# A decoder block on one core: the MLP split into an up phase and a down phase, the down projection by Strassen's seven block products

## What is computed

```python
x = x + rms_norm(mixed, norm_mix_post[l])
h2 = rms_norm(x, norm_mlp_pre[l])
a = jax.nn.relu(h2 @ w_up[l])                              # (512, 2048) @ (2048, 8192)
x = x + rms_norm((a * a) @ w_down[l], norm_mlp_post[l])    # (512, 8192) @ (8192, 2048)
```

## Time and profile before

| quantity | value |
|---|---|
| median of three executions | 2489.55 us |
| span of the profiled execution | 2488.2 us |
| TensorE busy | 2476.5 us, 100% of the span |
| TensorE granted clock, mean | 0.998 |
| VectorE busy | 1272.0 us, 51% |
| ScalarE busy | 679.9 us, 27% |
| GpSimd busy | 176.5 us, 7% |
| read from and written to HBM | 258.34 MB and 18.94 MB |

### The profile page before, as it was taken

One profiled execution on the slowest core, in us unless ns is written; L12 is line 12 of the kernel. 1 busy time (PEld: TensorE's weight loads), 2 busy tenths in 40 slices (PEclk: granted clock), 3 DMA queues, 4 the chain that ended last, 5 costly groups with the idle time before them and its releaser, 6 DMA issues.

```text
span 2488.2 us, 30616 instructions
## 1 busy us (share of the span) xinstructions
PE 2476.5 (100%) x11866; PEld 2024.4 (81%) x11866; DVE 1272.0 (51%) x1624; ACT 679.9 (27%) x909; POOL 176.5 (7%) x285
## 2 busy tenths in 40 slices
PE   9999999999999999999999999999999999999998
PEld 7866887877888888898888888888888888888887
DVE  8875688896434442264343443434344343434436
ACT  5145223333422222252122222212222221222223
POOL 1120334340000000000000000000000000000000
PEclk9999999999999999999999999999999999999999
DMA  6431333443434453343333322223332223333242
GB/s 225 109 115 51 114 119 108 130 123 102 134 96 142 148 177 98 111 160 103 101 102 102 101 93 93 89 97 101 101 101 93 93 89 97 101 101 101 93 159 101
DMA packets 83657, 278.34 MB, mean 112 GB/s; under 512 B 18016, under 2 KB 18080, under 8 KB 81536
## 3 DMA queue, kind: packets, MB, share of 16 engines
q1 hardware_dynamic: 64368, 233.34, 29.1%
q0 software_dynamic: 6544, 26.64, 3.2%
q10 hardware_dynamic: 12672, 17.34, 2.1%
HBM read 258.34 MB, written 18.94 MB: 111 GB/s over the span
## 4 chain that ended last, share of the span: by engine, by line
PE 98%; DVE 1%; ACT 0%; DMA 0%; issue 0%; DVEq 0%; ACTq 0%
PE main L1667 15%; PE main L1669 15%; PE main L1668 15%; PE side L1887 6%; PE side L1886 6%; PE side L1885 6%; PE main L1887 5%; PE main L1886 5%; PE main L1885 5%; PE side L1667 5%; PE side L1669 5%; PE side L1668 5%; PE side L1830 1%; PE side L1799 1%; PE side L1741 0%; PE side L1756 0%
## 5 line engine op out<-in xcount | busy, mean ns | idle before, releaser
L526 ACT ACTIVATE w_hi<-w_raw 128x1024 fp32r<-128x1024 f32 x435 | 452.5, 1056 | 1077.5 <-PE main L1669 401.0
L926 DVE TENSOR_TENSOR w_lo<-w_raw,w_hi 128x1024 fp32r<-128x1024 f32 x435 | 529.3, 1234 | 359.1 <-ACT w_hi L526 340.2
L1667 PE MATMUL main<-h_hi,w_hi 128*128 128x512 f32 x1280 | 505.4, 395 | 1.9 <-DVE h_lo L942 1.9
L1669 PE MATMUL main<-h_hi,w_lo 128*128 128x512 f32 x1280 | 499.4, 390 | 0.0
L1668 PE MATMUL main<-h_lo,w_hi 128*128 128x512 f32 x1280 | 498.9, 390 | 0.0
L1667 PEld LDWEIGHTS main<-h_hi,w_hi 128*128 128x128 f32 x1280 | 240.7, 188 | 56.3 <-issue 5.6
L1669 PEld LDWEIGHTS main<-h_hi,w_lo 128*128 128x128 f32 x1280 | 240.5, 188 | 50.7
L1668 PEld LDWEIGHTS main<-h_lo,w_hi 128*128 128x128 f32 x1280 | 240.9, 188 | 48.2 <-issue 0.2
L1667 PE MATMUL side<-h_hi,w_hi 128*128 128x512 f32 x512 | 199.2, 389 | 0.0
L1668 PE MATMUL side<-h_lo,w_hi 128*128 128x512 f32 x512 | 199.2, 389 | 0.0
L1669 PE MATMUL side<-h_hi,w_lo 128*128 128x512 f32 x512 | 199.2, 389 | 0.0
(11 more groups left out here) (353 smaller groups left out, 3139.9 us busy)
## 6 DMA issues: line engine op xcount, KB each, us to landing
w_raw<-wstream SPq DMA_DIRECT2D x435, 512.0 KB, 3.6
gate_scratch<-gate_stage ACTq DMA_DIRECT2D x16, 512.0 KB, 3.9
gate_attn<-gate_scratch POOLq DMA_DIRECT2D x8, 512.0 KB, 3.8
gate_ssm<-gate_scratch POOLq DMA_DIRECT2D x8, 512.0 KB, 4.5
x_rows<-x_rows POOLq DMA_DIRECT2D x4, 1024.0 KB, 11.8
x_scratch<-x_rows ACTq DMA_DIRECT2D x4, 1024.0 KB, 4.0
x_all<-x_scratch POOLq DMA_DIRECT2D x4, 1024.0 KB, 8.5
x<-x_t POOLq DMA_DIRECT2D x6, 512.0 KB, 6.3
```

The lines of the kernel that those rows point to most:

```text
L526: nc.scalar.activation(WH[:, s], RAW[:, s], ACT.Copy).then_inc(hi_ready, 1)
L926: tt(WL[:, s], RAW[:, s], WH[:, s].bitcast(F32), ALU.subtract).then_inc(lo_ready, 1)
L1667: mm(o, wh, xh[:, k0 + k], start=first and k == 0, stop=False)
L1669: ins = mm(o, wl, xh[:, k0 + k], start=False, stop=last and k == 3)
```

## The change

The MLP is split into two phases, and the hardware loops of the MLP are gone: all instructions are written out.

**Up phase.** The 128 units of `w_up` follow each other. After every four units (a *pair*: 256 hidden channels, all 512 tokens) VectorE writes the activations into `OPS[0:4]` (two blocks of 128 channels by two halves of 256 tokens), GpSimd builds five more blocks from sums and differences of these (`block_sums`), ScalarE and VectorE split the seven blocks that are needed into high and low parts in `STG`, and a DMA from GpSimd's queue stores them in DRAM (`a_scratch`, 1792 KB a pair, 32 pairs).

**Down phase.** It has 128 *sets*: 8 rounds (of 4 pairs of hidden blocks) x 2 halves of the output columns (`cb`, 1024 each) x 8, of which four sets (s//4 even, "first") make four products and four sets ("second") make three products. Together these are the seven products of Strassen's scheme for a 2x2 block product that would take eight: tokens in two halves, hidden channels in two halves of a pair, columns in two halves of 512. A product of a set is 6 matmuls of 512 columns (2 token blocks of 128 by 3), so a first set has 24 and a second set 18. Each product gathers over the four sets of its group in two PSUM banks; VectorE then adds it to one of seven slots of `ACC` (`gather`). The products need sums of weight blocks: GpSimd makes them in f32 (`weight_sums`, two of 128x512 in a first set, three in a second) before ScalarE and VectorE split them. The weights of a set come in one DMA of 768 KB (`weights_of`) into one of two buffers `RAWD`; `WHD` and `WLD` have two buffers too. The activations of a round come back from DRAM on ScalarE's queue (`load_first` 1024 KB, `load_second` 768 KB, four of each a round) while the second column half of the round before is being worked on.

**The end.** In the last round GpSimd does three block additions for each column half (`early`) and five gain products (`by_gain`), VectorE does five more block additions for each column half (`last_first`), and at the end VectorE adds the last three products, multiplies gains in, and writes the rows of two token blocks at a time (`rows_mean`, `rows_out`).

The diff, cut to what sets the order and the waits. The pieces behind the tables of products stand in the order SP, GpSimd, ScalarE, VectorE, TensorE.

```diff
+        S11, S12, S21, S22, S4, S5, S7 = range(7)
+        FIRST = ((0, 2, S21), (1, 1, S5), (2, 0, S12), (3, 3, S22))
+        SECOND = ((0, 0, S11), (1, 2, S4), (2, 1, S7))
...
+            for s in range(N_SET):
+                if s < 2:
+                    sp.wait_ge(lo_ready, N_UNIT - 2 + 2 * s)
+                else:
+                    sp.wait_ge(wd_sum, sums_until(s - 2))
+                    if is_first(s - 2):
+                        sp.wait_ge(wd_lo, 2 * s - 3)
+                sp.dma_start(RAWD[:, s % 2, weights_of(s)], wdown[s // 8, s % 4][:, weights_of(s)]
+                             ).then_inc(wd_landed[s % 2], 16)
...
+            def block_sums(k):
+                pool.wait_ge(a_ready, k + 1)
+                ptt(OPS[:, 4:6], OPS[:, 0:2], OPS[:, 2:4], ALU.add)
+                ptt(OPS[:, 6], OPS[:, 1], OPS[:, 0], ALU.subtract)
+                ptt(OPS[:, 7], OPS[:, 0], OPS[:, 3], ALU.add)
+                ptt(OPS[:, 8], OPS[:, 2], OPS[:, 3], ALU.subtract).then_inc(sums_ready, 1)
+                pool.wait_ge(ops_lo, k + 1)
+                pool.dma_start(a_dram[k], STG[:].bitcast(F32)).then_inc(a_stored, 16)
+            def weight_sums(s):
+                b12, b11, b22, b21 = (RAWD[:, s % 2, k] for k in range(4))
+                t0 = 3 * (s % 2)
+                pool.wait_ge(wd_landed[s % 2], 16 * (s // 2 + 1))
+                if s >= 2:
+                    pool.wait_ge(wd_lo, 2 * s - 2)
+                if is_first(s):
+                    ptt(TS[:, t0], b12, b22, ALU.subtract)
+                    ptt(TS[:, t0 + 1], b11, b12, ALU.add).then_inc(wd_sum, 1)
+                else:
+                    ptt(TS[:, t0], b11, b22, ALU.add)
+                    ptt(TS[:, t0 + 1], b21, b11, ALU.subtract).then_inc(wd_sum, 1)
+                    pool.wait_ge(wd_lo, 2 * s)
+                    ptt(TS[:, 2], b21, b22, ALU.add).then_inc(wd_sum, 1)
...
+            weight_sums(0)
+            weight_sums(1)
+            block_sums(N_PAIR - 1)
+            for s in range(2, N_SET):
+                weight_sums(s)
+                if s in (113, 114, 115, 121, 122, 123):
+                    early((s - 113) // 8, (s - 113) % 8)
+                if s >= 124:
+                    by_gain(0, s - 124, (S12, S22, S21, S11)[s - 124])
+            by_gain(1, 0, S12)
...
+            def down_hi(s, half):
+                if s < 2:
+                    act.wait_ge(unit_done, N_UNIT - 3 + 2 * s + half)
+                else:
+                    act.wait_ge(*used(s - 2, half))
...
+            def down_lo(s, half):
+                v.wait_ge(wd_hi, 2 * s + half + 1)
...
+                tt(WLD[:, s % 2, r], x, WHD[:, s % 2, r].bitcast(F32), ALU.subtract).then_inc(wd_lo, 1)
+            def gather(s, j):
+                k, slot = first_product(s) + j, products_of(s)[j][2]
+                o = ACC[:, s // 8 % 2, slot]
+                v.wait_ge(prod_done, k + 1)
...
+                    ins = tt(o, prod_banks(k), o, ALU.add)
+                ins.then_inc(prod_read, 1)
...
+            for s in range(N_SET):
+                last = s >= N_SET - 16
+                n = len(products_of(s))
+                for half, js in enumerate((range(0, 2), range(2, n))):
+                    for j in js if s % 4 == 3 else ():
+                        if last and not is_first(s):
+                            last_second(s // 8 % 2, j)
+                        else:
+                            if last and j == 3:
+                                v.wait_ge(early_ready, 3 * (s // 8 % 2) + 1)
+                            gather(s, j)
+                    if s + 2 < N_SET:
+                        down_lo(s + 2, half)
+                if last and s % 8 == 3:
+                    last_first(s // 8 % 2)
...
-            up(U_UP, B_UP, main, True)
-            up(U_MLP, B_MLP, up_banks(0), False)
-            down(U_MLP + 8, B_MLP + 2, 0, 0, 2)
-            with pe.Fori(0, (N_GROUP - 2) // 2) as i:
...
+            for s in range(N_SET):
+                n = len(products_of(s))
+                for j in range(n):
+                    k = first_product(s) + j
+                    if j in (0, 2):
+                        pe.wait_ge(wd_lo, 2 * s + j // 2 + 1)
+                    if j == 0 and s // 8 % 2 == 0:
+                        pe.wait_ge((ax_landed if is_first(s) else ay_landed)[s % 4], 16 * (s // 16 + 1))
+                    if s % 4 == 0 and k >= 4:
+                        pe.wait_ge(prod_read, k - 3)
+                    elif s % 4 == 0 and k >= 2:
+                        pe.wait_ge(bank_read, B_END + k - 3)
+                    ins = down_product(s, j, prod_banks(k))
```

494 lines of the change are left out of this document (268 added, 226 removed).

## The result

The changed kernel took 2518.22 us (median of 4 runs, 2517.52 to 2519.41), the kernel before 2489.53 in the same comparison: ratio 1.0116, 95% interval 1.0104 to 1.0128. It is slower by 1.2%, by more than what can be told from no change. The forecast was 2505 (2440 to 2535), with the chance of slower at 0.56.

What follows compares the result with a forecast made beforehand. TensorE was taken to bound the kernel. 2488.2 - 87.1 + 60 + 2 + 28 + 13 = 2504.1 us of span, plus 1.35 for the median of the runs, gave 2505 us, range 2440 to 2535.

Steps and rivals of the forecast that it cites:

- rival with two raw buffers: Down phase: two raw weight buffers are too few when activations share the DMA engines; 53 us, total 2532 us; chance 0.10.
- Matmuls removed, -87.1: Down projection on TensorE: 384 fewer matmuls at 0.2267 us each save 87.1 us.
- The price of a sum, 1.30: Down phase on GpSimd: one 128x512 sum of weight blocks takes 1.30 us, bounds 1.04 and 1.48.
- The weights' path, +60 (7.5 a round): Down phase: GpSimd's sums, stretched beside VectorE's low parts, come late; 7.5 us a round, +60 us in eight rounds.
- exclusion of the earlier trace: GpSimd operations and VectorE low parts exclude each other for all but the first 0.14 us of their time.
- first rival: Down phase: waits are short, with sums near 1.04 us or spare time of first sets fully used; 2455 us; chance 0.23.
- DMA at nothing: Down phase: reading weights and activations, 358 GB/s where both run, just fits the DMA engines and costs nothing.
- The sign named for it: Down phase: TensorE waiting for `ax_landed`, `ay_landed` or `wd_landed` would show the prediction wrong.
- Start of the down phase, +2: Start of the down phase: set 2's sums stand behind the last block sums; +2 us (0 to 5).
- Last round, +28: Last round: GpSimd's additions and gain products and VectorE's ten additions cost +28 us (15 to 33).
- The clock: Rival: TensorE's clock falls in waits, ten in the last round costing 15 us; it had no separate chance.
- The end, +13: After the last matmul: last additions, gain products, row updates and DMA take longer than before; +13 us (10 to 17).

Runs made afterwards that it cites:

- thin kernel: Changed kernel with each GpSimd sum of weight blocks from set 8 on made over 16 of 512 columns only (wrong output): 2437.19 us, ratio 0.979.
- fills of the same length: Changed kernel with GpSimd's weight sums from set 8 on replaced by memory fills that read nothing (wrong output): 2452.27 us, ratio 0.9853.
- start experiment: Changed kernel with gain rows loaded at set 20 and the sums of sets 2 and 3 ahead of the last store's wait: 2519.49 us, ratio 1.012.
- two edits of the last round: Changed kernel with GpSimd's six early additions moved to VectorE and its gain products put behind its last sums: 2515.07 us, ratio 1.0101.

## Why the prediction was right, and where its terms were off

The sign held, and so did the chain that carries the loss (matmuls gone, then GpSimd's sums late, stretched beside VectorE's low parts). The time came out 13 us above the forecast, halfway to the 2532 of the rival with two raw buffers, and the largest term came near for a reason that was only half right. By the prediction's steps:

- **Matmuls removed, -87.1.** Right: 0.2267 us between matmuls, 384 fewer, and in the thin kernel rounds of 336 x 0.2267 to the hundredth.
- **The price of a sum, 1.30**, continued from the earlier trace rows. Measured 1.28, on these rows of GpSimd ahead of the down phase:

```profile
1776.91 1.29 POOL L569 TENSOR_TENSOR wd_sums<-wd_raw 128x512 f32<-128x512 f32 x1
1778.17 1.28 POOL L570 TENSOR_TENSOR wd_sums<-wd_raw 128x512 f32<-128x512 f32 x1
```

The Trainium skill's figure (GPSIMD Engine Reference, section 3.1), 4497 ns for 2048 elements, gives an estimate of 1.12 by proportion. That is too low here, by the 1.28 measured.
- **The weights' path, +60 (7.5 a round).** Measured 8.5 a round over the bare matmuls, 68.1 in eight. This is the largest mis-sized term, and its make-up was wrong as well. The prediction put the 7.5 on the exclusion of the earlier trace rows alone and let the two raw buffers only limit how far GpSimd runs ahead. By itself what it names costs 2.8 a round, so that 7.5 came near 8.5 is in part luck. Runs with one of the two taken away show what each does:

| a round over the bare 76.16 us | two raw buffers | three raw buffers |
|---|---|---|
| sums (read and write) | 8.5 | 2.8 |
| fills of the same length | 1.1 (profiled run; 2.0 at the most) | not run |

Each alone costs 2.8 or 1.1, both together 8.5. Why they come to more than their sum is argued from the rows of after, not shown. In second sets a buffer is held, from the issue of its load to the end of its last sum, for 10.4 us on the mean in the first column half and 10.9 in the second (rounds 1 to 6), where two such sets last 8.16; 4.2 and 6.4 of that is the load. In first sets it is held for 10.8 and 10.1, where two sets last 10.9, so these have little to give. With sums of 1.28 us the second sets would be at 4.2 + 3.84 = 8.0 and 6.44 + 3.84 = 10.3: the first fits, the second doesn't quite. Idle time of GpSimd is no measure of this: it waited more for weights in the kernel with fills (129.5 us in rounds 1 to 6, in place of 101.8) and lost 1.1 us a round, since its own work was short. The bare port bound that the prediction gave for its first rival was 38.4 us in eight sets; three buffers come to 78.93 / 2 = 39.5, and the matmuls alone to 38.1.
- **DMA at nothing.** This step failed as it was put. The rate fits, as it said, but a load beside activations takes 6.4 to 6.6 us to land in place of 4.2, and that alone is 2.6 a round. The sign named for it couldn't show: TensorE's queue has no wait for `wd_landed`, and the wait sits three engines upstream, at GpSimd. The rival of two raw buffers named the place. Its load of 6.5 us was right for the sets beside activations; its cycle of 12.0 us measured 10.9, since the buffer was held for 4.5 us behind the landing and not 5.5. Its total of 53 was above the 40.4 that a third buffer gives back. Re-reading activations is 16.6 of loss when two buffers are used.
- **Start of the down phase, +2.** Round 0 lost 13.7 in place of 8.5, so 5.2, just above the stated 0 to 5. In the kernel with thin sums, where only sets 0 to 7 have whole sums, round 0 still lost 9.8, all of it in the products of these eight sets. The prediction's path missed a burst: the store of the last pair, the gain rows, and weights all together. In the windows of the changed kernel (busy us of each engine, then granted clock, DMA share, GB/s):

```profile
1795.00:1800.00 5.00, 2.34 (x11) 1.58 (x9) 2.16 (x1) 2.79 (x3) 4.12 (x4) 1.00 1.00 378
1800.00:1805.00 5.00, 4.74 (x21) 3.93 (x22) 2.48 (x3) 0.28 (x1) 0.00 (x0) 1.00 0.98 376
...
1810.00:1815.00 5.00, 2.05 (x5) 1.70 (x6) 4.96 (x4) 1.69 (x2) 5.00 (x4) 0.73 0.44 151
1815.00:1820.00 5.00, 5.00 (x14) 3.89 (x14) 3.59 (x5) 1.06 (x1) 4.37 (x4) 0.59 0.48 157
```

The DMA engines are full for 10 us and GpSimd (the fifth number with its count) does nothing from 1800 to 1805. Then TensorE waits 4.2 us, and behind that wait its clock is at the lower level, 1.2 GHz, for a dozen matmuls (granted clock 0.50 from 1813 to 1818). But the start experiment shows that mending this alone gives nothing.
- **Last round, +28.** 38.0 over bare, less the steady 8.5, is 29.5. Right in size and place: its longest waits are behind low parts and the gathers behind those, as the list of the last round's waits shows.

```profile
PE side L2161 <- DVE wd_lo L1712: 8.9, 2, 8.3
PE main L2161 <- DVE mlp_acc L1723: 6.4, 2, 5.8
PE side L2161 <- DVE mlp_acc L1723: 4.7, 2, 4.3
PE main L2161 <- DVE wd_lo L1712: 4.3, 1, 4.3
```

The parts, measured in kernels with three buffers: VectorE's ten additions 11.8, the place of the gain products 5.6, the six early additions 5.9 (3.0 when their new place is paid). The prediction had 10.8 for the first. They needn't add up to 29.5, and no run takes all three away.
- **The clock.** This rival came true in part, as a piece of the waits above and not beside them. In the down phase 67 matmuls start 0.43 us apart in place of 0.23: 13 in round 0, 14 in rounds 3 and 4, 40 in the last. That is 13.4 us, 8.0 of it in the last round, or less where TensorE would have waited later anyway. One stretch behind its longest wait but one (6.2 us between two starts), the columns as above:

```profile
2410.00:2415.00 5.00, 4.32 (x10) 3.46 (x11) 5.00 (x5) 0.63 (x2) 4.21 (x3) 0.50 0.49 157
```

- **The end, +13.** 21.4 us after the last matmul against the 8.6 of the earlier trace rows, so 12.8. The row updates took 1280 ns each, two groups of four.

```profile
2498.16 1.23 DVE L1782 TENSOR_TENSOR mlp_acc<-mlp_acc,gain_row_last 128x1024 f32<-128x1024 f32 x1
...
2500.95 4.87 DVE L1801 SCALAR_TENSOR_TENSOR mlp_acc<-mlp_acc,row_scalars,x_all 128x1024 f32<-128x1024 f32 x4
...
2507.39 4.87 DVE L1801 SCALAR_TENSOR_TENSOR mlp_acc<-mlp_acc,row_scalars,x_all 128x1024 f32<-128x1024 f32 x4
```

With measured sizes the sum is 2488.2 - 87.1 + 68.1 + 5.2 + 29.5 + 12.8 = 2516.7, against a span of 2516.0. Most of these sizes are differences taken from the same timeline, so the sum shows that nothing is left out, and not that each cause is right.

Still open: why the loss that is left with three buffers (2.8 us a round) stands at the gathers of the first sets alone, and how fills behave with three buffers. How much of the first round's 5.2 us is the burst, and how much the stored sums, can't be told, since both edits were made in one kernel.

## What to carry to other kernels

Before a bound engine's work is cut, write down for every producer in the chain both its time per step and the cycle of each buffer that feeds it (landing time plus the consumer's stretched time, against steps times buffers); an engine can lack slack in its buffers where it seems to have slack in its work. The wait that TensorE shows names the last link only: follow the queue of that engine upwards until an engine is found that is always busy, or waits for nothing but a load. Read landing times by stretch, too: one median (4.4 us here) can stand for loads of 4.2 and of 6.5. Where an engine has no time to spare, mending one late spot (the start, here) moves the wait and saves nothing; mend the rate first, and then the spots. The two edits of the last round gave 3.2 us together with two raw buffers and 9.2 with three.
